# Two of the four weight sums of a feed-forward pair made by adding DMAs from GpSimd

## The chip, the cores and the metric

The kernel runs on one core of one Trainium2 chip. The metric is the device time of one execution in microseconds (us), the median of several runs. The core has TensorE (PE in the rows) for matmuls, VectorE (DVE), ScalarE (ACT), GpSimd (POOL) and SyncE (SP), each with an instruction stream of its own that runs in order; semaphores tie them together. DMAs are issued by SP or, where the text says so, by POOL.

## The reference

A block of layers on x of shape (1, 256, 1024): a first model with two layers (an "even" and an "odd" attention mixer, each followed by a feed-forward network), then one layer of a second model, again with a feed-forward network. The change touches the three feed-forward networks only. Cut to them:

```
D_MODEL, SEQ, D_FF = 1024, 256, 2816        # float32 throughout

def swiglu(h, w1, w3, w2):
    return (jax.nn.silu(h @ w1) * (h @ w3)) @ w2

# layers 0 and 1 of the first model
h = rms_norm(x, norm_ffn_g[layer])
x = x + swiglu(h, ffn_w1[layer], ffn_w3[layer], ffn_w2[layer])
# the layer of the second model
h2 = rmsnorm(x, norm2_w)
x = x + (jax.nn.silu(h2 @ w_ffn_gate) * (h2 @ w_ffn_up)) @ w_ffn_down
```

## The kernel before

**Three products for one.** Every float32 matmul is made as three fp32r matmuls: a weight block W is split into `high` (W rounded to fp32r, written by ScalarE, L719 from the ring `raw` or L724 from a block in `arena`) and `low` (W minus high, written by VectorE, L1167 or L1173), and `three_products` (L1779 to L1781) adds x_high·W_high, x_high·W_low and x_low·W_high. A weight block, a "unit", is 128 partitions x 2048 values, 1 MB, loaded by two DMAs of 512 KB. `high` and `low` have three slots each (RING = 3): the high of a unit may be written when TensorE has done the unit three places ahead of it in the order, and TensorE starts a unit when its low is there (`low_ready`).

**A feed-forward network** has 11 hidden chunks of 256 columns. Chunks 0, 1, 2, 5 and 8 are "plain": two up units U (24 matmuls each). Chunks (3,4), (6,7) and (9,10) are pairs, the FIRST, MIDDLE and LAST one. For a pair the product of two row tiles of x with two chunks, over two halves of the inner dimension, is a 2x2 by 2x2 block product, made with seven products of 12 matmuls each (Winograd's form of Strassen's algorithm) in place of eight. The four weight blocks of a pair are B11 and B12 (upper half of the inner dimension, chunks p and p+1) and B21 and B22 (lower half). They are loaded into X11, X12, X21 and X22 in `arena`, and VectorE makes four sums of them, T1 = B12-B11 (L1337, `t1`), T2 = B22-T1 (L1346, `t2`), T4 = B21-T2 (L1351, `t4`) and T3 = B22-B12 (L1357, `t3`), each over 128 x 2048 values, in the tiles XT1 and XT2. Product P1 uses B11, P2 B21, P3 B22, P4 T4, P5 T1, P6 T2 and P7 T3. Every hidden chunk c also has a down unit D(c) (24 matmuls) with the transpose `hiddenT` of its hidden values ahead of it (ScalarE L833, VectorE L1311).

**What sets the order.** `ffn_order` (L75) gives the order of units for all engines, and each engine's program is written out by hand in that order: `pair_begin`, `pair_end` and `last_pair_end` exist for ScalarE, VectorE and TensorE. On TensorE a pair runs P1, D, P5, D, P6, P2, P3, then U, P7, U, P4; the MIDDLE pair has a further D behind P6, and the LAST pair has no U: it runs P7, D, P4, D, D. Behind a product, ScalarE and VectorE take pieces of the result out of PSUM: `s1` and `s5` copies, `u2` (L1378), `c12` (L1383), `silu_c11` (ScalarE L864) with `gate_c11` (VectorE L1399). The U behind a pair writes the PSUM banks 0 and 1, so TensorE starts its first half only after `gate_c11` and its second after `c12` (`up_after_pair`).

**Loads.** SP issues all weight loads in one written order (`load_ffn`); the loads of the next pair into X11, X21, X12 and X22 each wait for the last reader of the tile. GpSimd issues a few small loads early, and computes reciprocal roots between the networks; during the feed-forward networks it does nothing.

Of the kernel before, what the change touches and what calls it, by code (L numbers as in the profile page):

```python
# [32 lines left out]
P = 128  # L33
# [107 lines left out]
def program(nc, x, norm_mix_g, norm_ffn_g, ev_w_in, ev_w_out, ev_q_norm_g, ev_k_norm_g, ev_pool_w,  # L141
# [59 lines left out]
    with ExitStack() as ctx:  # L201
# [84 lines left out]
        X11, X12, X22, X21, XT1, XT2 = (take(UNIT) for _ in range(6))  # L286
# [82 lines left out]
        x11_in, x12_in, x22_in, x21_in = sem("x11_in"), sem("x12_in"), sem("x22_in"), sem("x21_in")  # L369
        x_copied = sem("x_copied")  # L370
# [157 lines left out]
        def _(sp):  # L528
# [33 lines left out]
            def load_ffn(f):  # L562
# [11 lines left out]
                up_quarter(f, X12, p + 1, 0, x12_in)  # L574
# [4 lines left out]
                for p in PAIRS[:-1]:  # L579
# [54 lines left out]
        def _(pool):  # L634
# [42 lines left out]

            row_rstd(0, 0)
# [10 lines left out]
            for e in (1, 2, 3, 4):  # L689
# [5 lines left out]
                load_gain(NORMS[e + 1], e + 1)  # L695
            head_rstd((4, 5, 6, 7), 8)
# [8 lines left out]
            row_rstd(6, 5)  # L705


        @block.scalar
        def _(act):
# [106 lines left out]
            def ffn(f):  # L816
# [39 lines left out]
                def high_t(p, i):  # L856

                    src, made = {5: (XT1, 1), 6: (XT2, 2), 4: (XT2, 4 if p == LAST_PAIR else 3), 7: (XT1, 3 if p == LAST_PAIR else 4)}[i]
                    act.wait_ge(t_ready, 4 * pair_seq(f, p) + made)
                    block_high(n0 + FFN_AT["P", p, i], src)  # L860
# [9 lines left out]
                def pair_begin(p):  # L870
# [4 lines left out]
                    high_t(p, 5)  # L875
# [6 lines left out]
                    high_t(p, 6)  # L882
                    pair_product_done(p, 5)
                    nc.scalar.activation(f_C22, bank(1), ACT.Copy).then_inc(s5_ready, 1)
                    if p == MIDDLE_PAIR:
                        down(w[2])
                        hiddenT(w[2])
                    high_b21(p)
                    if p == LAST_PAIR:
                        hiddenT(w[2])  # L890
                    high_b22(p)

                def pair_end(p):
# [3 lines left out]
                    high_t(p, 7)  # L897
                    up(p + 2, 1)
                    silu_of(p, f_C12, c12_ready)
                    high_t(p, 4)  # L900
# [6 lines left out]
                def last_pair_end(p):  # L907

                    high_t(p, 7)
                    silu_c11(p)  # L910
                    down(p - 3)
                    high_t(p, 4)
# [247 lines left out]
        def _(dve):  # L1160
# [134 lines left out]
            def ffn(f):  # L1295
# [24 lines left out]
                def low_of(p, i):  # L1320

                    src = {1: X11, 2: X21, 3: X22, 4: XT2, 5: XT1, 6: XT2, 7: XT1}[i]
# [9 lines left out]
                def t1(p):  # L1332
                    dve.wait_ge(x11_in, 32 * pair_seq(f, p) + 32)
                    dve.wait_ge(x12_in, 32 * pair_seq(f, p) + 32)
                    if p > FIRST_PAIR:
                        low_done(p - 3, 7)
                    nc.vector.tensor_tensor(XT1, X12, X11, ALU.subtract).then_inc(t_ready, 1)  # L1337

                def t2(p):
                    dve.wait_ge(x22_in, 32 * pair_seq(f, p) + 32)  # L1340
                    dve.wait_ge(t_ready, 4 * pair_seq(f, p) + 1)
# [4 lines left out]
                    nc.vector.tensor_tensor(XT2, X22, XT1, ALU.subtract).then_inc(t_ready, 1)  # L1346

                def t4(p):
                    dve.wait_ge(x21_in, 32 * pair_seq(f, p) + 32)
                    low_done(p, 6)  # L1350
                    nc.vector.tensor_tensor(XT2, X21, XT2, ALU.subtract).then_inc(t_ready, 1)  # L1351

                def t3(p):

                    dve.wait_ge(t_ready, 4 * pair_seq(f, p) + 2)
                    low_done(p, 5)
                    nc.vector.tensor_tensor(XT1, X22, X12, ALU.subtract).then_inc(t_ready, 1)  # L1357
# [1007 lines left out]
```

## Time and profile before

| | |
|---|---|
| runs | 971.13, 971.67, 971.86 us; median 971.67 |
| the profiled execution | 972.1 us, span from first to last instruction 970.3 us |
| TensorE busy | 960.7 us, 99% of the span, 4644 matmuls; granted clock 1.0 throughout |
| VectorE busy | 761.3 us, 78% |
| ScalarE busy | 546.5 us, 56% |
| GpSimd busy | 42.8 us, 4% |
| DMA | 177.48 MB, 183 GB/s in the mean |

The profile shows one execution. "Busy" of TensorE counts a matmul of 512 columns as some 0.39 us, while the next one starts 0.227 us after it, so short waits hide inside the busy share; a wait of TensorE is read from the distance of two starts. The three networks run at about 95 to 269, 388 to 563 and 792 to 967 us. The three show the same pattern to 0.01 us at the places spoken of below, so rows are shown of the first one.

### The profile page before, as it was taken

The numbers are of one execution on the slowest core, as the hardware profiler recorded it, in microseconds if no ns is written. First come the engines' busy times: TensorE is split into PE (matmuls) and PEld (weight loads), VectorE is DVE, ScalarE is ACT, GpSimd is POOL, SyncE is SP. The second block draws the span as 40 slices with busy tenths as digits, with TensorE's granted clock in tenths as the row PEclk, the third lists the DMA queues.
The fourth block names the chain that finished last, engine by engine and source line by source line (L and its number), as shares of the span: only waits on it lengthen the run. The fifth ranks groups of instructions, "written<-read, shape, count | busy, mean of one in ns | idle before, by whom it ended". The sixth has DMA issues, their size and how long they took to land.

```text
span 970.3 us, 11764 instructions
## 1 busy us (share of the span) xinstructions
PE 960.7 (99%) x4644; PEld 788.8 (81%) x4644; DVE 761.3 (78%) x790; ACT 546.5 (56%) x579; POOL 42.8 (4%) x62
## 2 busy tenths in 40 slices
PE   8999999999999999999999999999999999999998
PEld 6878888888788888888888788888888888888886
DVE  5978879899865777879999885963565678899896
ACT  6556655656555755655555655555344465565662
POOL 2511000000000000000000021000000000000000
PEclk9999999999999999999999999999999999999999
DMA  8643966472374434967472275446435559456511
GB/s 298 256 131 114 354 230 224 149 242 87 107 239 154 149 111 130 314 224 264 132 260 87 87 240 179 168 149 199 154 127 197 165 183 341 155 199 215 187 74 44
DMA packets 112473, 177.48 MB, mean 183 GB/s; under 512 B 6817, under 2 KB 74529, under 8 KB 112418
## 3 DMA queue, kind: packets, MB, share of 16 engines
q1 hardware_dynamic: 110992, 172.73, 53.3%
q0 software_dynamic: 1280, 3.94, 1.2%
q8 instruction: 37, 0.61, 0.3%
q14 instruction: 18, 0.15, 0.0%
q10 hardware_dynamic: 146, 0.07, 0.0%
HBM read 175.66 MB, written 1.05 MB: 182 GB/s over the span
## 4 chain that ended last, share of the span: by engine, by line
PE 85%; DVE 9%; issue 3%; ACT 3%; POOL 0%; DMA 0%; DVEq 0%; ACTq 0%
PE psum L1779 26%; PE psum L1781 25%; PE psum L1780 25%; PE psum L1851 4%; DVE low L1173 4%; DVE low L1167 1%; ACT high L724 1%; DVE arena L1357 1%; DVE arena L1351 1%; DVE arena L1566 1%; PE psum L2183 1%; DVE small L1565 1%; PE psum L1868 1%; ACT high L719 1%; PE psum L2214 1%
## 5 line engine op out<-in xcount | busy, mean ns | idle before, releaser
L1167 DVE TENSOR_TENSOR low<-raw,high 128x2048 fp32r<-128x2048 f32 (+1 forms) x123 | 277.3, 2258 | 106.1 <-ACT high L719 106.0
L1779 PE MATMUL psum<-high,xh 128*128 128x512 f32 x732 | 291.0, 398 | 0.0
L1781 PE MATMUL psum<-high,xl 128*128 128x512 f32 x732 | 285.6, 390 | 0.0
L1780 PE MATMUL psum<-low,xh 128*128 128x512 f32 x732 | 285.1, 390 | 0.0
L719 ACT ACTIVATE high<-raw 128x2048 fp32r<-128x2048 f32 (+1 forms) x125 | 236.2, 1890 | 75.0 <-PE psum L1781 74.1
L1781 PEld LDWEIGHTS psum<-high,xl 128*128 128x128 f32 x732 | 137.4, 188 | 29.4
L1779 PEld LDWEIGHTS psum<-high,xh 128*128 128x128 f32 x732 | 137.5, 188 | 28.3 <-issue 0.7
L1780 PEld LDWEIGHTS psum<-low,xh 128*128 128x128 f32 x732 | 137.7, 188 | 26.8
L1173 DVE TENSOR_TENSOR low<-arena,high 128x2048 fp32r<-128x2048 f32 x63 | 144.0, 2286 | 15.1 <-ACT high L724 15.1
L724 ACT ACTIVATE high<-arena 128x2048 fp32r<-128x2048 f32 x63 | 120.6, 1914 | 43.4 <-PE psum L1781 43.4
L1779 PE MATMUL psum<-high,mh 128*128 128x512 f32 x256 | 103.8, 406 | 1.4 <-DVE low L1173 1.4
L1779 PE MATMUL psum<-high,gh 128*128 128x512 f32 x264 | 103.6, 392 | 0.4
L1781 PE MATMUL psum<-high,gl 128*128 128x512 f32 x264 | 102.9, 390 | 0.0
L1780 PE MATMUL psum<-low,gh 128*128 128x512 f32 x264 | 102.8, 389 | 0.0
L1781 PE MATMUL psum<-high,ml 128*128 128x512 f32 x256 | 100.2, 391 | 0.0
L1780 PE MATMUL psum<-low,mh 128*128 128x512 f32 x256 | 99.8, 390 | 0.0
L833 ACT ACTIVATE gh<-psum 128x512 fp32r<-128x512 f32 x33 | 19.8, 599 | 82.2 <-PE psum L1851 81.8
L1779 PEld LDWEIGHTS psum<-high,mh 128*128 128x128 f32 x256 | 48.1, 188 | 14.1 <-issue 5.0
L1779 PEld LDWEIGHTS psum<-high,gh 128*128 128x128 f32 x264 | 49.6, 188 | 11.7 <-DVE gl L1311 1.6
L1781 PEld LDWEIGHTS psum<-high,gl 128*128 128x128 f32 x264 | 49.6, 188 | 10.4
L1780 PEld LDWEIGHTS psum<-low,gh 128*128 128x128 f32 x264 | 49.6, 188 | 10.1
L1781 PEld LDWEIGHTS psum<-high,ml 128*128 128x128 f32 x256 | 48.0, 188 | 10.7
(183 smaller groups left out, 890.2 us busy)
## 6 DMA issues: line engine op xcount, KB each, us to landing
raw<-in_ffn_w SPq DMA_DIRECT2D x84, 512.0 KB, 5.0
raw<-in_w_in SPq DMA_DIRECT2D x52, 512.0 KB, 4.6
arena<-in_ffn_w SPq DMA_DIRECT2D x48, 512.0 KB, 5.6
raw<-in_od_w_qkv SPq DMA_DIRECT2D x24, 512.0 KB, 4.8
raw<-in_w_ffn_down SPq DMA_DIRECT2D x22, 512.0 KB, 4.5
raw<-in_ev_w_in SPq DMA_DIRECT2D x12, 512.0 KB, 6.4
arena<-in_w_ffn_gate SPq DMA_DIRECT2D x12, 512.0 KB, 5.1
arena<-in_w_ffn_up SPq DMA_DIRECT2D x12, 512.0 KB, 6.1
```

Source lines behind the costliest of these rows:

```text
L719: nc.scalar.activation(high[:, n % RING, 0:cols], raw[:, r, 0:cols], ACT.Copy).then_inc(high_ready, 1)
L724: nc.scalar.activation(high[:, n % RING, :], src, ACT.Copy).then_inc(high_ready, 1)
L833: nc.scalar.activation(gh[:, s % 2], bank(6).rearrange("p (k n) -> p k n", k=2), ACT.Copy).then_inc(gh_ready, 1)
L1167: nc.vector.tensor_tensor(low[:, n % RING, 0:cols], raw[:, RING_AT[n] % RING, 0:cols], high[:, n % RING, 0:cols].bitcast(F32), ALU.subtrac ...
L1173: nc.vector.tensor_tensor(low[:, n % RING, :], src, high[:, n % RING, :].bitcast(F32), ALU.subtract).then_inc(low_ready, 1)
L1351: nc.vector.tensor_tensor(XT2, X21, XT2, ALU.subtract).then_inc(t_ready, 1)
L1357: nc.vector.tensor_tensor(XT1, X22, X12, ALU.subtract).then_inc(t_ready, 1)
L1565: step(nc.vector.max(top8, score))
L1779: nc.tensor.matmul(out, sh, wh, start=start, stop=False, skip_group_check=True)
L1780: nc.tensor.matmul(out, sh, wl, start=False, stop=False, skip_group_check=True)
L1781: return nc.tensor.matmul(out, sl, wh, start=False, stop=stop, skip_group_check=True)
L1851: ins = nc.tensor.transpose(bank(dst_bank, j * P, (j + 1) * P), src, ident)
```

## The change

Of the four sums of a pair VectorE makes two, T2 and T4. T1 and T3 are made by DMAs that GpSimd issues with an adding write: B12 is loaded into XT1 and B11 is added to it from HBM; later, when B22 in X22 has been split for P3 and read for T2, B12 is added to it from HBM, and X22 then holds T3. The signs are turned so that all are sums (T1 = B11+B12, T3 = B22+B12, T2 = B22+T1, T4 = B21+T2), with the signs of the x sums and of the two combining steps c12 and c22 turned to match. The tile X12 is gone. As X22 has to be done with before T3 can be made, P3 comes ahead of P6 and P2: the order is P1, D, P5, D, P3, P2, P6 in the FIRST pair, P3, P2, D, P6 in the MIDDLE pair, and P3, P6, P2 in the LAST pair. SP's load order changes too: X22 of the next pair now waits for the low of P7.

```diff
         w = [("D", c) for c in downs_within(p)]
-        order += [("P", p, 1), w[0], ("P", p, 5), w[1], ("P", p, 6)] + [d for d in w[2:] if p == MIDDLE_PAIR]
-        order += [("P", p, 2), ("P", p, 3)]
+        order += [("P", p, 1), w[0], ("P", p, 5), w[1], ("P", p, 3)]
+        if p == FIRST_PAIR:
+            order += [("P", p, 2), ("P", p, 6)]
+        elif p == MIDDLE_PAIR:
+            order += [("P", p, 2), w[2], ("P", p, 6)]
+        else:
+            order += [("P", p, 6), ("P", p, 2)]
...
-        X11, X12, X22, X21, XT1, XT2 = (take(UNIT) for _ in range(6))
+        X11, X22, X21, XT1, XT2 = (take(UNIT) for _ in range(5))
...
                     load_up(f, p + 2, 0)
-                    after_low("P", p, 5)
+                    load_up(f, p + 2, 1)
+                    after_low("D", p - 1)
                     up_quarter(f, X11, p + 3, 0, x11_in)
-                    load_up(f, p + 2, 1)
+                    up_quarter(f, XT1, p + 4, 0, x12_in)
                     load_down(f, p + 1)
-                    after_low("P", p, 2)
+                    after_low("U", p + 2, 0)
                     up_quarter(f, X21, p + 3, 1, x21_in)
-                    after_low("P", p, 3)
-                    up_quarter(f, X12, p + 4, 0, x12_in)
                     load_down(f, p + 2)
+                    after_low("P", p, 7)
                     up_quarter(f, X22, p + 4, 1, x22_in)
                     load_down(f, p)
...
+            def add_quarter(f, c, block, done):
+
+                block = block.rearrange("p (k c) -> p k c", k=4)
+                for j in range(2):
+                    src = FFN_W[f][j][0:4 * P, c * FC:(c + 1) * FC]
+                    pool.dma_start(block[:, :, j * FC:(j + 1) * FC], src.rearrange("(k p) c -> p k c", p=P), accum_op=ALU.add
+                                   ).then_inc(done, 16)
+
+            def ffn_sums(f):
+                n0 = U_FFN[f]
+                for p in PAIRS:
+                    pool.wait_ge(x12_in, 32 * pair_seq(f, p) + 32)
+                    add_quarter(f, p, XT1, t1_in)
+                    pool.wait_ge(low_ready, n0 + FFN_AT["P", p, 3] + 1)
+                    pool.wait_ge(t_ready, 2 * pair_seq(f, p) + 1)
+                    add_quarter(f, p + 1, X22, t3_in)
...
+                def high_t3(p):
+                    act.wait_ge(t3_in, 32 * pair_seq(f, p) + 32)
+                    block_high(n0 + FFN_AT["P", p, 7], X22)
...
-                nc.vector.tensor_tensor(XT1, X12, X11, ALU.subtract).then_inc(t_ready, 1)
...
-                nc.vector.tensor_tensor(XT1, X22, X12, ALU.subtract).then_inc(t_ready, 1)
```

On VectorE, in the FIRST pair of a network, from the transpose behind D(2) on. L1173 and L1214 are the low of a pair block, L1167 and L1208 the low of a ring unit (here the U behind the pair), L1351 and L1385 are T4, L1357 is T3, L1399 and L1427 `gate_c11`, L1378 and L1406 `u2`. Before:

```order
L1311 TENSOR_TENSOR gl<-psum,gh 128x512
L1173 TENSOR_TENSOR low<-arena,high 128x2048
L1351 TENSOR_TENSOR arena<-arena 128x2048
L1173 TENSOR_TENSOR low<-arena,high 128x2048
L1357 TENSOR_TENSOR arena<-arena 128x2048
L1173 TENSOR_TENSOR low<-arena,high 128x2048
L1167 TENSOR_TENSOR low<-raw,high 128x2048
L1399 SCALAR_TENSOR_TENSOR xn<-psum,small,xn 128x256
L1378 TENSOR_TENSOR xn<-psum,arena 128x512
```

After:

```order
L1352 TENSOR_TENSOR gl<-psum,gh 128x512
L1214 TENSOR_TENSOR low<-arena,high 128x2048 x3
L1385 TENSOR_TENSOR arena<-arena 128x2048
L1208 TENSOR_TENSOR low<-raw,high 128x2048
L1427 SCALAR_TENSOR_TENSOR xn<-psum,small,xn 128x256
L1406 TENSOR_TENSOR xn<-psum,arena 128x512
```

The lows of P3, P2 and P6 now stand in a row, and T4, which stood behind the first low, stands behind all three, right ahead of the low of the U unit and of `gate_c11`.

On VectorE in the LAST pair, from the low of the third product on (L1387 and L1415 are `u3`). Before:

```order
L1173 TENSOR_TENSOR low<-arena,high 128x2048
L1357 TENSOR_TENSOR arena<-arena 128x2048
L1173 TENSOR_TENSOR low<-arena,high 128x2048
L1351 TENSOR_TENSOR arena<-arena 128x2048
L1311 TENSOR_TENSOR gl<-psum,gh 128x512
L1173 TENSOR_TENSOR low<-arena,high 128x2048
L1378 TENSOR_TENSOR xn<-psum,arena 128x512
L1173 TENSOR_TENSOR low<-arena,high 128x2048
L1399 SCALAR_TENSOR_TENSOR xn<-psum,small,xn 128x256
L1167 TENSOR_TENSOR low<-raw,high 128x2048
L1387 TENSOR_TENSOR xn<-psum,arena 128x512
```

After:

```order
L1214 TENSOR_TENSOR low<-arena,high 128x2048 x2
L1352 TENSOR_TENSOR gl<-psum,gh 128x512
L1214 TENSOR_TENSOR low<-arena,high 128x2048
L1385 TENSOR_TENSOR arena<-arena 128x2048
L1406 TENSOR_TENSOR xn<-psum,arena 128x512
L1214 TENSOR_TENSOR low<-arena,high 128x2048
L1427 SCALAR_TENSOR_TENSOR xn<-psum,small,xn 128x256
L1208 TENSOR_TENSOR low<-raw,high 128x2048
L1415 TENSOR_TENSOR xn<-psum,arena 128x512
```

T3 is gone, the lows of P3 and P6 come first, and the low of P2, T4 and `u2` stand between them and the low of P7 (the last L1214).

On GpSimd, behind the reciprocal roots ahead of the first network. Before:

```order
L693 DMA cst<-consts 128x1536
L638 DMA gains<-in_norm_mix_g 128x1024
L650 TENSOR_SCALAR small<-small 128x1
```

After (with the semaphores waited for):

```order
L716 DMA cst<-consts 128x1536 [waits pooled_ready]
L644 DMA gains<-in_norm_mix_g 128x1024 [waits xn_ready]
L689 DMA arena<-in_ffn_w 128x4x256 [waits x12_in]
L689 DMA arena<-in_ffn_w 128x4x256
L689 DMA arena<-in_ffn_w 128x4x256 [waits t_ready,low_ready]
L689 DMA arena<-in_ffn_w 128x4x256
```

Twelve adding DMAs per network are new: two for T1 and two for T3 in each of three pairs.

## Rows read from the trace of the kernel before

**Rows 1.** The page: busy us of each engine (share of the span) xinstructions.

```profile
PE 960.7 (99%) x4644; PEld 788.8 (81%) x4644; DVE 761.3 (78%) x790; ACT 546.5 (56%) x579; POOL 42.8 (4%) x62
```

**Rows 2.** Waits of PE: us in total, times, longest.

```profile
PE psum L1779 <- DVE low L1173: 1.4, 6, 0.3
```

**Rows 3.** Groups by line, VectorE: busy us, mean ns, idle before.

```profile
L1357 DVE TENSOR_TENSOR arena<-arena 128x2048 f32<-128x2048 f32 x9 | 20.6, 2285 | 0.0
```

**Rows 4.** Timeline of PE, FIRST pair: start us, us.

```profile
152.89 0.39 PE L1781 MATMUL psum<-high,xl 128*128 128x512 f32 x1
153.56 0.47 PE L1779 MATMUL psum<-high,mh 128*128 128x512 f32 x1 [0.28 <-DVE low L1173]
...
156.40 0.39 PE L1779 MATMUL psum<-high,xh 128*128 128x512 f32 x1
```

**Rows 5.** Timeline of DVE, FIRST pair.

```profile
142.12 2.29 DVE L1173 TENSOR_TENSOR low<-arena,high 128x2048 fp32r<-128x2048 f32 x1 [1.12 <-ACT high L724]
144.51 2.29 DVE L1351 TENSOR_TENSOR arena<-arena 128x2048 f32<-128x2048 f32 x1
...
151.12 2.28 DVE L1173 TENSOR_TENSOR low<-arena,high 128x2048 fp32r<-128x2048 f32 x1
153.33 2.28 DVE L1167 TENSOR_TENSOR low<-raw,high 128x2048 fp32r<-128x2048 f32 x1
155.53 0.48 DVE L1399 SCALAR_TENSOR_TENSOR xn<-psum,small,xn 128x256 f32<-128x256 f32 x1
```

**Rows 6.** Timeline of ACT, FIRST pair.

```profile
140.17 1.91 ACT L724 ACTIVATE high<-arena 128x2048 fp32r<-128x2048 f32 x1
...
142.93 1.91 ACT L724 ACTIVATE high<-arena 128x2048 fp32r<-128x2048 f32 x1
147.93 1.92 ACT L724 ACTIVATE high<-arena 128x2048 fp32r<-128x2048 f32 x1 [3.09 <-PE psum L1781]
```

**Rows 7.** Timeline of PE, LAST pair.

```profile
238.06 0.48 PE L1779 MATMUL psum<-high,mh 128*128 128x512 f32 x1
...
240.90 0.39 PE L1779 MATMUL psum<-high,xh 128*128 128x512 f32 x1
...
243.97 0.47 PE L1779 MATMUL psum<-high,mh 128*128 128x512 f32 x1 [0.19 <-DVE low L1173]
...
249.61 0.39 PE L1779 MATMUL psum<-high,gh 128*128 128x512 f32 x1
```

**Rows 8.** Timeline of ACT, LAST pair.

```profile
232.96 1.91 ACT L724 ACTIVATE high<-arena 128x2048 fp32r<-128x2048 f32 x1
...
238.34 0.60 ACT L833 ACTIVATE gh<-psum 128x512 fp32r<-128x512 f32 x1 [3.47 <-PE psum L1851]
238.84 1.91 ACT L724 ACTIVATE high<-arena 128x2048 fp32r<-128x2048 f32 x1
```

**Rows 9.** Timeline of DVE, LAST pair.

```profile
243.75 0.68 DVE L1378 TENSOR_TENSOR xn<-psum,arena 128x512 f32<-128x512 f32 x1
244.35 2.28 DVE L1173 TENSOR_TENSOR low<-arena,high 128x2048 fp32r<-128x2048 f32 x1
```

**Rows 10.** Timeline of SP: DMA issues; then DMAs issued at 149 to 150, us to landing.

```profile
149.03 0.93 SPq L548 DMA_DIRECT2D arena<-in_ffn_w  x2
...
arena<-in_ffn_w SPq DMA_DIRECT2D x2, 512.0 KB, 4.5
```

**Rows 11.** Windows: length, PE, PEld, DVE, ACT, POOL busy, PEclk, DMA share, GB/s.

```profile
153.50:154.00 0.50, 0.45 (x2) 0.43 (x3) 0.50 (x1) 0.50 (x2) 0.00 (x0) 1.00 0.33 102
...
235.00:240.00 5.00, 5.00 (x26) 4.14 (x25) 5.00 (x3) 1.66 (x2) 0.00 (x0) 1.00 0.01 6
```

**Rows 12.** Timeline of POOL: two DMA issues.

```profile
25.00 0.81 POOL L670 DMA_DIRECT2D poolw<-in_ev_pool_w  x1
...
93.55 0.63 POOL L693 DMA_DIRECT2D cst<-consts  x1
```

**Rows 13.** Timeline of DVE beside the second of them.

```profile
93.14 2.28 DVE L1167 TENSOR_TENSOR low<-raw,high 128x2048 fp32r<-128x2048 f32 x1
```

More of the change, by code:

```diff
@@ L705, in _ @@
             row_rstd(6, 5)
+            ffn_sums(2)
         @block.scalar
@@ L854, in high_b22, with high_t1, high_t2, high_t4 @@
                     block_high(n0 + FFN_AT["P", p, 3], X22)
[L856 to L860, printed above, removed]
+                def high_t1(p):
+                    act.wait_ge(t1_in, 32 * pair_seq(f, p) + 32)
+                    block_high(n0 + FFN_AT["P", p, 5], XT1)
+                def high_t3(p):
+                    act.wait_ge(t3_in, 32 * pair_seq(f, p) + 32)
+                    block_high(n0 + FFN_AT["P", p, 7], X22)
+                def high_t2(p):
+                    act.wait_ge(t_ready, 2 * pair_seq(f, p) + 1)
+                    block_high(n0 + FFN_AT["P", p, 6], XT2)
+                def high_t4(p):
+                    act.wait_ge(t_ready, 2 * pair_seq(f, p) + 2)
+                    block_high(n0 + FFN_AT["P", p, 4], XT2)
                 def silu_c11(p):
@@ L1345, in t2 @@
                         dve.wait_ge(sums_low, f + 1)
-                    nc.vector.tensor_tensor(XT2, X22, XT1, ALU.subtract).then_inc(t_ready, 1)
+                    nc.vector.tensor_tensor(XT2, X22, XT1, ALU.add).then_inc(t_ready, 1)
                 def t4(p):
@@ L1350, in t4 @@
                     low_done(p, 6)
[L1351 to L1356, printed above, removed]
-                    nc.vector.tensor_tensor(XT1, X22, X12, ALU.subtract).then_inc(t_ready, 1)
+                    nc.vector.tensor_tensor(XT2, X21, XT2, ALU.add).then_inc(t_ready, 1)
                 def x_sums():
@@ L1367, in x_sums @@
                     dve.wait_ge(prep_step, at + 4)
-                    nc.vector.tensor_tensor(a22, a21, a22, ALU.add).then_inc(prep_step, 1)
+                    nc.vector.tensor_tensor(a22, a21, a22, ALU.subtract).then_inc(prep_step, 1)
                     nc.vector.tensor_tensor(a21, a11, a21, ALU.subtract).then_inc(prep_step, 1)
@@ L1372, in x_sums @@
                     dve.wait_ge(prep_step, at + 7)
-                    nc.vector.tensor_tensor(a12, a12, a11, ALU.subtract).then_inc(prep_step, 1)
+                    nc.vector.tensor_tensor(a12, a12, a11, ALU.add).then_inc(prep_step, 1)
                 def u2(p):
@@ L1382, in c12 @@
                     dve.wait_ge(u2_ready, pair_seq(f, p) + 1)
-                    nc.vector.tensor_tensor(f_C12, bank(1), f_C12, ALU.add).then_inc(c12_ready, 1)
+                    nc.vector.tensor_tensor(f_C12, bank(1), f_C12, ALU.subtract).then_inc(c12_ready, 1)
                 def u3_and_c22(p):
@@ L1389, in u3_and_c22 @@
                     dve.wait_ge(s5_ready, pair_seq(f, p) + 1)
-                    nc.vector.tensor_tensor(f_C22, f_C21, f_C22, ALU.add).then_inc(c22_ready, 1)
+                    nc.vector.tensor_tensor(f_C22, f_C22, f_C21, ALU.subtract).then_inc(c22_ready, 1)
                 def c21(p):
@@ L1966, in pair_begin, with product_2, product_6 @@
                         hiddenT(w[2])
-                        pe.wait_ge(c21_ready, g)
-                    product(p, 6, bank(7), sum_tile(2), True, False)
-                    if p == MIDDLE_PAIR:
-                        down(w[2])
-                    pe.wait_ge(s1_ready, g + 1)
-                    product(p, 2, bank(0), x_tile(0, 1), False, True)
                     pe.wait_ge(s5_ready, g + 1)
                     product(p, 3, bank(1), sum_tile(4), False, True)
+                    if p == LAST_PAIR:
+                        product_6(p)
+                        product_2(p)
+                    else:
+                        product_2(p)
+                        if p == MIDDLE_PAIR:
+                            down(w[2])
+                        product_6(p)
+                def product_2(p):
+                    pe.wait_ge(s1_ready, pair_seq(f, p) + 1)
+                    product(p, 2, bank(0), x_tile(0, 1), False, True)
+                def product_6(p):
+                    if p > FIRST_PAIR:
+                        pe.wait_ge(c21_ready, pair_seq(f, p))
+                    product(p, 6, bank(7), sum_tile(2), True, False)
                 def product_7(p):
```

75 lines of the change are left out of this document (34 added, 41 removed).

## The prediction

> **What bounds the kernel now.** I read the page first: TensorE is busy 960.7 of 970.3 us, VectorE 761.3, ScalarE 546.5, GpSimd 42.8 [rows 1]. So no time is to be had but what TensorE waits. The waits list gives its waits for weight lows: six, 1.4 us together, and all on VectorE's L1173 [rows 2]. Since a matmul counts as 0.39 us of busy time but the next starts 0.227 us after it, I took the cost from the timeline of starts. In the FIRST pair the last matmul of P2 starts at 152.89, P3 only at 153.56: 0.44 us more than the step of 0.227, and P3 then takes 2.84 us (to 156.40) where 12 steps are 2.72, another 0.12 for starting up after a wait [rows 4]. In the LAST pair P2 starts at 240.90 and P3 at 243.97, 3.07 where 2.72 would do: 0.35 us [rows 7]. Both come back in each of the three networks (hence six waits). All that the change can win in the pairs is thus 0.56 + 0.47 or so per network, 3.1 us in all, however much work leaves VectorE. What matters is whether the new order makes TensorE wait elsewhere.
>
> **What is removed.** T1 and T3 leave VectorE: 18 instructions, of which the nine of T3 take 2.285 us each, 20.6 us [rows 3]; those of T1 have the same shape. That is about 41 us of VectorE, but beside TensorE's work: directly it is worth only the waits above. The turned signs change no instruction's count or shape: nothing.
>
> **The FIRST pair after the change.** TensorE's times up to the end of D(2) stay as they are, since the order up to there does. D(2) is done at 147.93, which is when ScalarE may write the high of the third unit behind it [rows 6]. Before, that unit was P2; now it is P6. I follow the chain with the steps that the rows show. High of P6: 147.93 + 1.92 = 149.85. VectorE starts a low 0.04 after the high (140.17 + 1.91 to 142.12) [rows 5, 6]: 149.89. T4 overwrites the block just read, so it waits for that low to be complete: it starts 2.39 us behind it (142.12 to 144.51) [rows 5], at 152.28. The low of the next U starts 2.21 later, at 154.49, and gate_c11 2.20 later, at 156.69, and takes 0.48 (steps 151.12, 153.33, 155.53) [rows 5]: 157.17. U writes bank 0, which gate_c11 reads, so TensorE starts it some 0.16 us behind that (as P3 started at 153.56 behind a low that ended at 153.40) [rows 4, 5]: at 157.33. Without a wait TensorE would have been there at 152.89 + 0.23 (end of the second product behind D(2)) + 2.72 = 155.84 [rows 4]. P3 itself no longer waits: its high takes the place at 142.93 [rows 6], its low is over by 147.2, half a microsecond ahead of TensorE. But U waits, 1.5 us. Before, U started at 156.40 [rows 4]: 0.93 us later now, and 0.12 for starting up behind a wait: **+1.05 us**. What is queued behind T4 on VectorE is just what TensorE asks for next; before the change T4 stood two instructions earlier, in a gap. The work behind this place (u2, c12, low of P7) ends by 160.8, TensorE is at P7 at about 162.9: no second wait.
>
> **The MIDDLE pair.** D(3) stands between P2 and P6, another 5.4 us of cover. The same counting gives the low of U(8,0) ready some 1.8 us ahead of TensorE. Nothing.
>
> **The LAST pair.** P7 follows straight on the three products. TensorE would reach it at 238.06 + 2.84 + 2 x 2.72 = 246.34 [rows 7]. Its low needs two things.
> One is VectorE's queue. The high of P2 stands behind the copy of a transpose (238.34) and is written from 238.84 to 240.75, as before [rows 8]; low of P2 from 240.79, T4 from 243.0, u2 from 245.2, and the low of P7 0.60 behind u2 (243.75 to 244.35) [rows 9], at 245.8. It ends at 248.1 and P7 starts at 248.25: a wait of 1.9 us even if T3 is there in time. T4 sits ahead of a low that TensorE needs first; before, the low of P7 followed u2 at 244.35 and its product followed P3 unhindered.
> The other is T3. Its adding DMAs may start when the low of P3 is made: high from 232.96 to 234.87 [rows 8], low to 237.2. Call the lag the time from there to the landing of both DMAs; the high and low of P7 and the step to TensorE then add 0.04 + 1.92 + 0.04 + 2.28 + 0.16 = 4.44. P7 starts at the later of 248.25 and 241.64 plus the lag; the first holds up to a lag of 6.6.
>
> **The lag of an adding DMA pair** is in no row. Near end: the same 1 MB as plain loads from SP, two DMAs issued in 0.93 us from 149.03, with 4.5 us to landing each, traffic falling off at 153.5 to 154.0 [rows 10, 11], so about 5.0 us; GpSimd needs 0.81 us to issue one DMA of 128 x 4 pieces [rows 12] where SP needs less, 2 x 0.81 - 0.93 = 0.7 us more for the pair: a lag of 5.7. Far end: an adding write has to fetch the old value too, so the engines would move every byte twice; the stretch of traffic in the rows was some 3.8 us long (149.03 plus about a microsecond to its fall-off), and a second 3.8 gives 9.5. Below 5.7 it cannot go, as nothing makes the adding kind cheaper than the plain one. At 235 to 240 the DMA engines are idle (share 0.01) [rows 11], so no queue is added. I take 8, nearer to the far end, since the second fetch goes through the same engines. P7 then starts at 249.6, and D(6) 2.84 later, at 252.5, where it was 249.61 [rows 7]: **+2.9 us**. D(6)'s own high follows T3's on ScalarE and its low is over at about 252.1, just ahead. Behind it the order is unchanged and the delay passes on to the end.
>
> **The rest of the adding DMAs.** T1 has long cover: B12 of the FIRST pair lands at about 115, T1's high is written at 131.5 and T2 at 135.6; in the other pairs the distance is over 15 us. T3 of the FIRST pair may start at 147.2 and is needed for a high by about 158, of the MIDDLE one more. The 18 MB more of traffic fall mostly into gaps, but 100 to 128 us is full already, so D(1), X22 and D(2) land later by up to 4 us; their users come 5 us or more after them before. I put nothing on it and keep it for the upper end.
>
> The page "SBUF — State Buffer" of the Trainium skill (the box on how VectorE blocks DMAs of GpSimd) says that GpSimd cannot write its descriptors while VectorE runs an instruction that takes both ports, and that a tensor_tensor takes only the read side. In this trace GpSimd issued a DMA at 93.55 in 0.63 us in the middle of a VectorE low that ran from 93.14 to 95.42 [rows 12, 13]: no blocking seen, which agrees with the second half. By the first half alone, the issue at 237.2 would wait for the low of P6 behind it; that case is priced below.
>
> **Sum.** Per network 1.05 + 2.86 = 3.9, times three 11.7 us; the profiled execution of 972.1 would become 983.8. The median of the runs is 0.4 below the profiled one, so **983.4 us**.
>
> **Rivals.**
> (a) T3 lands within 6.6 us. VectorE's queue sets P7, and D(6), whose high stands behind silu_c11 of the now later P2, costs 0.3 more: 1.05 + 1.8 per network, 980.2. For it: the near end. Against: the second fetch. Chance 0.14.
> (b) Forecast, a lag from 6.6 to 9.5: 980.2 to 987.9. Chance 0.58.
> (c) Blocking by VectorE: GpSimd's issue waits for a low, 2.2 us more of lag in each LAST pair, 6.6 us in all: 990. Against it stands the issue at 93.55 [rows 12, 13]. Chance 0.05. The page of the Trainium skill named above is where a blocking of this kind is described.
> (d) The adding write is slow by itself, with a lag of 12. LAST pair +6.9; in the FIRST pair P7 would wait as well, 147.2 + 12 + 4.4 = 163.6 against 162.9: 0.7. With 1.05 that is 8.6 per network, 26 us: 997. Nothing speaks for it but that no row shows such a DMA. Chance 0.14.
> (e) The other side: faster. If VectorE, with 41 us taken off, had run ahead at both places, only the old waits would go: 3.1 us, 968.6. It decides on whether the low of P7 in the LAST pair ends by 246.2; the chain above puts it at 248.1, and its start is tied to TensorE's own D(8), not to VectorE's load, so lighter load does not help. Chance 0.04.
> (f) About no change: one of the two waits is as I say and the other is not there. Chance 0.05.
>
> **How the numbers follow.** The likeliest is (b), 983.4. The range from 978.5 (a with a microsecond and a half of error) to 992 (c, and part of d) leaves out (e), (f) and most of (d). About 0.2% is what a measurement of this kernel can tell from no change. Slower by more: a, b, c, d, 0.91; within: 0.05; faster: 0.04.
>
> **What would show it.** In the profile after: VectorE's busy time about 41 us less; TensorE waiting at the U behind the FIRST pair's P6 for gate_c11, 1.5 us, and at P7 of the LAST pair, 1.9 us or more, three times each; no wait at P3. The DMAs on GpSimd's queue show the lag directly. If P7's wait ends with VectorE's queue, it is (a); if ScalarE idles until the DMA lands, (b) to (d). I am wrong if P7 of the LAST pair does not wait, or if TensorE waits near the start of a network for D(1), T1 or X22.

## The result: slower by 2.1%, nearly twice what was forecast

| | before | after |
|---|---|---|
| median | 971.63 us (971.13 to 971.86) | 992.69 us (990.33 to 993.32) |
| profiled execution | 972.1 us, span 970.3 us | 993.3 us, span 991.5 us |

The ratio is 1.0214 (95% interval 1.0202 to 1.0226). The forecast was 983.4 us, 11.7 us more than before, with a range up to 992.0; measured are 21.1 us more. The direction and the two places were right; the size was not, and the median lies 0.7 us above the range.

**The page of the kernel after**: the span, busy us of each engine, and two of its lines in 40 slices.

```profile
span 991.5 us, 11773 instructions
...
PE 966.9 (98%) x4644; PEld 793.8 (80%) x4644; DVE 724.1 (73%) x772; ACT 545.8 (55%) x579; POOL 90.1 (9%) x98
...
PEclk9999999999899999999999899999999999999999
```

VectorE lost 37.2 us of busy time against [rows 1] and the kernel is longer by 21. TensorE has the same 4644 matmuls and 6.2 us more of busy time. That is strange for equal work, and the clock line gives the reason: in two slices it stands at 8 where the clock was full throughout before.

**The waits of TensorE after**: us in total, times, longest.

```profile
PE psum L1797 <- DVE low L1214: 12.5, 3, 4.3
PE psum L1797 <- DVE xn L1427: 4.0, 3, 1.3
```

The six short waits of [rows 2] have become three of 4 us and three of 1.3 us. They are the two places of the prediction, once each in every network.

**The FIRST pair after**, timeline of TensorE (start us, us). It runs 0.19 us ahead of the trace of before at the start of the first network, so 0.19 is to be added when the two are compared.

```profile
155.42 0.39 PE L1799 MATMUL psum<-high,ml 128*128 128x512 f32 x1
157.13 0.47 PE L1797 MATMUL psum<-high,xh 128*128 128x512 f32 x1 [1.32 <-DVE xn L1427]
```

And VectorE at that place:

```profile
149.70 2.29 DVE L1214 TENSOR_TENSOR low<-arena,high 128x2048 fp32r<-128x2048 f32 x1 [0.53 <-ACT high L752]
152.10 2.29 DVE L1385 TENSOR_TENSOR arena<-arena 128x2048 f32<-128x2048 f32 x1
154.31 2.29 DVE L1208 TENSOR_TENSOR low<-raw,high 128x2048 fp32r<-128x2048 f32 x1
156.51 0.48 DVE L1427 SCALAR_TENSOR_TENSOR xn<-psum,small,xn 128x256 f32<-128x256 f32 x1
```

TensorE's last matmul of P6 starts at 155.42 and U at 157.13, 1.71 us later instead of 0.227: a wait of 1.48. T4 (L1385) stands ahead of the low of U and of `gate_c11` (L1427), and TensorE waits for the latter. The U starts 0.92 us later than in [rows 4], the 0.19 counted in, and with 0.11 for starting up behind the wait, all that follows it comes 1.03 us later.

**The LAST pair after**, ScalarE and GpSimd from the low of P3 on:

```profile
239.68 1.91 ACT L752 ACTIVATE high<-arena 128x2048 fp32r<-128x2048 f32 x1
247.25 1.91 ACT L752 ACTIVATE high<-arena 128x2048 fp32r<-128x2048 f32 x1 [5.67 <-DMA arena<-in_ffn_w]
```

```profile
238.32 2.57 POOL L689 DMA_DIRECT2D arena<-in_ffn_w  x2 [39.59 <-DVE low L1214]
```

VectorE there:

```profile
235.74 4.49 DVE L1214 TENSOR_TENSOR low<-arena,high 128x2048 fp32r<-128x2048 f32 x2 [3.12 <-ACT high L752]
...
241.62 2.29 DVE L1214 TENSOR_TENSOR low<-arena,high 128x2048 fp32r<-128x2048 f32 x1 [0.79 <-ACT high L752]
243.82 2.28 DVE L1385 TENSOR_TENSOR arena<-arena 128x2048 f32<-128x2048 f32 x1
246.03 0.68 DVE L1406 TENSOR_TENSOR xn<-psum,arena 128x512 f32<-128x512 f32 x1
249.19 2.29 DVE L1214 TENSOR_TENSOR low<-arena,high 128x2048 fp32r<-128x2048 f32 x1 [2.48 <-ACT high L752]
```

The first of the two lows that start at 235.74 (P3's) is over at 238.02. GpSimd begins to issue T3's two adding DMAs at 238.32 and needs 2.57 us for it. ScalarE stands still until they have landed, at 247.25: a lag of 9.2 us. VectorE is done with `u2` at 246.7 and waits too, so it is not its queue that sets P7 but the DMA.

TensorE there:

```profile
246.95 0.39 PE L1799 MATMUL psum<-high,xl 128*128 128x512 f32 x1
251.63 0.77 PE L1797 MATMUL psum<-high,mh 128*128 128x512 f32 x1 [4.29 <-DVE low L1214]
...
253.05 0.63 PE L1797 MATMUL psum<-high,mh 128*128 128x512 f32 x1
...
254.33 0.63 PE L1797 MATMUL psum<-high,mh 128*128 128x512 f32 x1
...
256.89 0.63 PE L1797 MATMUL psum<-high,gh 128*128 128x512 f32 x1
```

P7 starts at 251.63, after a wait of 4.45 us (4.39 and 4.18 in the other two networks). The part that the prediction does not have comes next. From 253.05 to 254.33 there are three matmuls, 0.43 us each, where the step was 0.227. P7 takes 5.26 us, to 256.89, and not 2.84. The windows over this stretch (length; PE, PEld, DVE, ACT, POOL busy; PEclk; DMA share; GB/s) say why:

```profile
245.00:250.00 5.00, 2.34 (x11) 1.60 (x9) 2.52 (x3) 2.75 (x3) 0.00 (x0) 1.00 0.34 54
250.00:252.50 2.50, 0.87 (x2) 0.80 (x3) 2.50 (x3) 2.50 (x2) 0.00 (x0) 0.64 0.00 0
252.50:255.00 2.50, 2.50 (x7) 1.92 (x7) 1.57 (x1) 0.62 (x1) 0.00 (x0) 0.50 0.00 0
255.00:257.50 2.50, 2.50 (x7) 1.92 (x7) 0.37 (x1) 0.00 (x0) 0.00 (x0) 0.50 0.80 244
257.50:260.00 2.50, 2.50 (x13) 2.04 (x12) 2.47 (x4) 1.24 (x3) 0.00 (x0) 0.99 0.45 175
```

TensorE's granted clock (PEclk) is full (1.00, that is 2.4 GHz) up to 250, falls while the engine stands waiting for P7, stays at 0.50 (1.2 GHz) until about 257.5 and is full again from there. The Trainium skill ("TensorE: Matmul & The Clock Gate", Part 1: The HAM clock gate) gives this clock gate two states, 1.2 and 2.4 GHz, with the lower one for an idle engine and 426.7 ns from start to start of 512 columns there; the trace agrees, with 0.43 us.

**Where the 21 us are.** Read from the distances between TensorE's starts, in the LAST pair from the first matmul of the three products into D(6), summed over the three networks:

| | us |
|---|---|
| FIRST pair, wait for `gate_c11` and starting up (3 x 1.03) | 3.1 |
| LAST pair, as forecast with a lag of 8 (3 x 2.86) | 8.6 |
| LAST pair, P7 later than that (1.15, 1.1, 0.9) | 3.1 |
| P7 and the start of D(6) at half clock (2.75, 2.3, 1.6) | 6.6 |
| sum; difference of the spans | 21.4; 21.2 |

The last two rows are what the forecast lacked. The last one was a claim so far: the half clock could also be there without the wait. The experiments were made for that, and for the lag.

### The profile page after: what moved, and what is told of

Same layout as the page of the kernel before. It is cut to its first block, busy times and chain, and to the rows that moved or that the text cites. A ratio compares the mean times of both kernels' runs of the same rounds, so it can differ in the third digit from the quotient of the medians.

```text
span 991.5 us, 11773 instructions
## 1 busy us (share of the span) xinstructions
PE 966.9 (98%) x4644; PEld 793.8 (80%) x4644; DVE 724.1 (73%) x772; ACT 545.8 (55%) x579; POOL 90.1 (9%) x98
## 3 DMA queue, kind: packets, MB, share of 16 engines
HBM read 194.53 MB, written 1.05 MB: 197 GB/s over the span
## 4 chain that ended last, share of the span: by engine, by line
PE 85%; DVE 7%; ACT 3%; DMA 3%; issue 1%; POOL 1%; ACTq 0%; DVEq 0%
PE psum L1797 26%; PE psum L1799 25%; PE psum L1798 25%; PE psum L1869 4%; DVE low L1214 2%; DVE low L1208 2%; ACT high L752 2%; DMA arena<-in_ffn_w 2%; DMA arena<-in_w_ffn_up 1%; DVE arena L1584 1%; PE psum L2212 1%; DVE small L1583 1%; PE psum L1886 1%; ACT high L747 1%; PE psum L2243 1%
## 5 line engine op out<-in xcount | busy, mean ns | idle before, releaser
L1208 DVE TENSOR_TENSOR low<-raw,high 128x2048 fp32r<-128x2048 f32 (+1 forms) x123 | 277.3, 2258 | 106.7 <-ACT high L747 106.6
L1214 DVE TENSOR_TENSOR low<-arena,high 128x2048 fp32r<-128x2048 f32 x63 | 143.5, 2290 | 58.7 <-ACT high L752 58.6
L1797 PE MATMUL psum<-high,mh 128*128 128x512 f32 x256 | 106.0, 414 | 12.5 <-DVE low L1214 12.5
L1798 PE MATMUL psum<-low,mh 128*128 128x512 f32 x256 | 102.4, 400 | 0.0
L1799 PE MATMUL psum<-high,ml 128*128 128x512 f32 x256 | 102.3, 400 | 0.0
L1799 PEld LDWEIGHTS psum<-high,gl 128*128 128x128 f32 x264 | 49.7, 188 | 10.5
```

What stands on the lines that cost most here:

```text
L1208: nc.vector.tensor_tensor(low[:, n % RING, 0:cols], raw[:, RING_AT[n] % RING, 0:cols], high[:, n % RING, 0:cols].bitcast(F32), ALU.subtrac ...
L1214: nc.vector.tensor_tensor(low[:, n % RING, :], src, high[:, n % RING, :].bitcast(F32), ALU.subtract).then_inc(low_ready, 1)
L1797: nc.tensor.matmul(out, sh, wh, start=start, stop=False, skip_group_check=True)
L1798: nc.tensor.matmul(out, sh, wl, start=False, stop=False, skip_group_check=True)
L1799: return nc.tensor.matmul(out, sl, wh, start=False, stop=stop, skip_group_check=True)
```

## The experiments

Each is compared with the kernel before, timed beside it on the same chip (971.26 or 971.32 us). The diffs are against the kernel after.

### No adding DMAs in the LAST pair

```diff
                     pool.wait_ge(low_ready, n0 + FFN_AT["P", p, 3] + 1)
+                    if p == LAST_PAIR:
+                        continue
...
                 def high_t3(p):
-                    act.wait_ge(t3_in, 32 * pair_seq(f, p) + 32)
+                    if p < LAST_PAIR:
+                        act.wait_ge(t3_in, 64 * f + 32 * PAIRS.index(p) + 32)
```

> The changed kernel without the two adding DMAs of T3 in the LAST pair of each network (P7 there uses B22 instead of T3: that part of the computation is left out). Theory: the wait of 4.4 us ahead of P7 is the lag of these DMAs (9.2 us from the low of P3 to landing), and behind them stands VectorE's queue (low of P2, T4, u2) at 1.9 us. So P7's wait falls to 1.9 us, not to nothing. If TensorE's clock stays at full speed after so short a wait, the time is 971.6 + 3 x (1.05 + 1.6) = 979.6 us; if it falls as it does after 4.4 us, some 8 us more, 987.5. Rival (the adding DMAs cost something elsewhere, P7's wait is VectorE's): the wait stays above 3 us and the time above 989.

Measured: 979.57 us, ratio 1.0087 (1.0072 to 1.0102). Its waits of TensorE, and P7's start in the first network:

```profile
PE psum L1800 <- DVE low L1217: 5.2, 3, 1.7
PE psum L1800 <- DVE xn L1430: 4.0, 3, 1.3
```

```profile
246.07 0.39 PE L1802 MATMUL psum<-high,xl 128*128 128x512 f32 x1
248.18 0.47 PE L1800 MATMUL psum<-high,mh 128*128 128x512 f32 x1 [1.72 <-DVE low L1217]
248.49 0.40 PE L1801 MATMUL psum<-low,mh 128*128 128x512 f32 x1
```

With T3 never late, P7 still waits, 2.11 - 0.227 = 1.88 us: this is VectorE's queue (low of P2, T4, `u2`), which the prediction put at 1.9. The mean clock is 1.0 and the steps behind the wait are 0.23 again. So the adding DMAs of this one pair cost 13.1 us in three networks (992.69 - 979.57), the half clock included. The other 8.3 us over the kernel before are the FIRST pair's 3.1 and some 1.8 per network in the LAST pair: the wait of 1.88, another of 0.22 ahead of D(6), less the 0.35 that P3 used to wait.

### The same DMAs as plain writes

```diff
-            def add_quarter(f, c, block, done):
+            def add_quarter(f, c, block, done, add=True):
...
-                    pool.dma_start(..., accum_op=ALU.add
+                    pool.dma_start(..., **({"accum_op": ALU.add} if add else {})
...
-                    add_quarter(f, p + 1, X22, t3_in)
+                    add_quarter(f, p + 1, X22, t3_in, add=p < LAST_PAIR)
```

> The changed kernel with T3's two DMAs of the LAST pair as plain writes from the same queue instead of adding ones (P7 there uses B12 instead of T3: the addition is left out). Theory: a part of the lag of 9.2 us is the second fetch of the adding write; the plain pair lands some 2.5 to 3.5 us sooner (lag 5.7 to 6.7), P7's wait falls from 4.4 to about 2 us, and the time is as that of the run without these DMAs, 980 to 988 us depending on the clock. Rival (the lag is the issue by GpSimd, 2.6 us, and the load itself; adding costs nothing): the lag stays above 8.5 us and the time at 992 to 993.

Measured: 980.35 us, ratio 1.0095 (1.008 to 1.011). GpSimd's issue and the high of P7 in the first network, and from the DMA view of 238 to 241 us the time to landing:

```profile
238.38 1.55 POOL L689 DMA_DIRECT2D arena<-in_ffn_w  x2 [40.13 <-DVE low L1214]
```

```profile
244.16 1.92 ACT L752 ACTIVATE high<-arena 128x2048 fp32r<-128x2048 f32 x1 [2.52 <-DMA arena<-in_ffn_w]
```

```profile
arena<-in_ffn_w POOLq DMA_DIRECT2D x2, 512.0 KB, 4.7
```

The same view of the kernel after has

```profile
arena<-in_ffn_w POOLq DMA_DIRECT2D x2, 512.0 KB, 7.2
```

The low of P3 ends at 238.07 here and the block is there at 244.16: a lag of 6.1 us. The near end of the prediction, 5.7 from SP's loads and an issue of 0.81 per DMA, was good for the plain kind. Adding makes it 9.2. GpSimd needs 2.57 instead of 1.55 us to issue the pair, but data already flows while it issues, so this delays the start of the traffic by only 0.5 us (from 239.75 to 240.25). The other 2.5 us are a longer transfer: the traffic lasts from 240.25 to 246.5 where the plain pair's lasts from 239.75 to 243.5. One microsecond from the middle of each, the adding pair first (columns as in the windows above):

```profile
242.00:243.00 1.00, 1.00 (x6) 0.84 (x5) 1.00 (x1) 0.00 (x0) 0.00 (x0) 1.00 1.24 199
```

```profile
242.00:243.00 1.00, 1.00 (x6) 0.82 (x5) 1.00 (x1) 0.00 (x0) 0.00 (x0) 1.00 1.01 344
```

The DMA engines are no less busy and move 199 GB/s in place of 344. That fits the second fetch of the prediction, but the fetch itself is in no trace. The two kinds also differ in their packets, 1056 against 288 for the same 1 MB; SP's plain pair of [rows 10] has 1055 packets and runs at some 385 GB/s, so their number alone does not halve the rate on SP's queue.

The other thing to read here is that a lag of 6.1 costs nothing in the LAST pair: it is as long as with no DMA at all (to 0.04 us), since VectorE's queue holds P7 back as long. P7 again waits 1.88 us, at full clock. Between the two traces there are 0.8 us as between the medians, and all of them lie ahead of the first network, which the edit does not touch. The step from here to the kernel after, 3.1 us of lag, costs 12.3 us.

### TensorE kept running through the wait

```diff
                 def last_pair_end(p):
+                    pe.wait_ge(gl_ready, down_seq(f, p - 3) + 1)
+                    for i in range(18):
+                        nc.tensor.matmul(bank(6), xh[:, 0, 0:P], xh[:, 2 * (i % 4):2 * (i % 4) + 2, :].rearrange("p k n -> p (k n)"),
+                                         start=True, stop=True, skip_group_check=True)
                     product_7(p)
```

> The changed kernel with 18 matmuls of no use (512 columns each, into a bank that is free) ahead of P7 in the LAST pair of each network, 18 x 0.227 = 4.1 us, while TensorE would wait for T3. Theory: the half clock behind the wait (0.43 us a matmul for 12 to 14 matmuls) comes from TensorE having stood still; kept busy it stays at full clock, P7 starts at the same time, and the loss of 2.9, 2.7 and 2.0 us in the three networks goes: 992.7 - 7.6 = 985 us. Rival (the clock falls for another reason, as the DMAs or the place in the program): the half clock stays, and the time is 992 to 994.

Measured: 985.64 us (985.21 to 986.13), ratio 1.0149 (1.0134 to 1.0164). Timeline of TensorE and a window of the same place (this trace runs 1.15 us ahead of the one of after):

```profile
246.02 4.24 PE L2023 MATMUL psum<-xh 128*128 128x512 f32 x18
250.25 0.47 PE L1797 MATMUL psum<-high,mh 128*128 128x512 f32 x1
...
253.06 0.39 PE L1797 MATMUL psum<-high,gh 128*128 128x512 f32 x1
```

```profile
250.00:252.50 2.50, 2.50 (x12) 1.92 (x11) 2.50 (x3) 1.74 (x1) 0.00 (x0) 1.00 0.00 0
```

This is the run that settles the clock. P7 starts as late as in the kernel after (0.2 us earlier, counted from the start of the pair, in two networks and 0.2 later in the third), VectorE, ScalarE and the DMAs do the same work, and 54 matmuls whose result nobody uses have been added. Yet it is 7.05 us shorter, because P7 now takes 2.81 us (250.25 to 253.06; 2.84 and 2.81 in the other networks) and not 5.26, 5.14 and 4.41. The table above had 6.6 for this. The half clock is thus a result of TensorE's standing still, and it is a third of the whole loss.

### T4 of the FIRST pair behind `c12`

```diff
+                    sp.wait_ge(t_ready, 2 * pair_seq(f, p) + 2)
                     up_quarter(f, X21, p + 3, 1, x21_in)
...
                         low_of(p, 6)
-                        t4(p)
+                        if p > FIRST_PAIR:
+                            t4(p)
...
                     c12(p)
+                    if p == FIRST_PAIR:
+                        t4(p)
                     low_of(p, 7)
```

> The changed kernel with T4 of the FIRST pair moved on VectorE from ahead of the U unit's low to behind c12, ahead of the low of P7 (SP's load into X21 waits for it). Theory: the wait of TensorE ahead of the U unit, 1.5 us with 0.1 for starting up, three times, is T4 in front of the U's low and gate_c11; it goes, and nothing is late in its place: 992.7 - 3 x 1.6 = 987.9 us. Rival: something else is late by nearly as much (low of P7 or the reload of X21), the wait moves and the time stays above 991.

Measured: 990.28 us (988.71 to 991.78), ratio 1.0191 (1.0174 to 1.0208): the median is 2.4 us below that of after, half of what was expected. The runs of the two kernels overlap (988.7 to 991.8 against 990.3 to 993.3), so the size of the gain is known only roughly; what the edit does is read from the trace. The waits and the FIRST pair of its first network:

```profile
PE psum L1801 <- DVE low L1215: 14.5, 6, 4.1
```

```profile
159.84 0.39 PE L1803 MATMUL psum<-high,xl 128*128 128x512 f32 x1
161.32 0.47 PE L1801 MATMUL psum<-high,mh 128*128 128x512 f32 x1 [1.09 <-DVE low L1215]
```

The wait of U for `gate_c11` is gone from the list, so its cause is shown: T4's place. But a wait of 1.25 us (0.79 in the other networks) stands one unit later, at P7 of the FIRST pair. T3 is late there as well. In the kernel after that was hidden, since U came late itself: the low of P7 is over at 161.99 there and P7 starts at 162.68. These are GpSimd and ScalarE of the kernel after:

```profile
147.27 2.55 POOL L689 DMA_DIRECT2D arena<-in_ffn_w  x2 [29.58 <-DVE low L1214]
150.35 2.56 POOL L689 DMA_DIRECT2D arena<-in_ffn_w  x2 [0.53 <-DMA arena<-in_ffn_w]
```

```profile
157.75 1.92 ACT L752 ACTIVATE high<-arena 128x2048 fp32r<-128x2048 f32 x1 [4.15 <-DMA arena<-in_ffn_w]
```

T3 is issued at 147.27 and ScalarE has it at 157.75, 10.5 us later. The windows over the two lags (columns as before) show what is different:

```profile
147.50:157.50 10.00, 8.68 (x39) 6.92 (x38) 9.37 (x6) 4.32 (x3) 4.88 (x4) 1.00 1.18 257
238.00:247.00 9.00, 9.00 (x44) 7.39 (x42) 7.92 (x6) 2.40 (x2) 2.57 (x2) 1.00 0.78 117
```

In the FIRST pair the DMA engines move 257 GB/s, SP's loads and GpSimd's next pair (from 150.35) among them, in the LAST one 117, nothing but T3. So of the 1.6 us per network that U's wait and start had cost, 1.25 are lost again at P7 in the first network and 0.79 in the others. In the LAST pair this kernel is slower: P7 takes 5.26, 5.25 and 5.26 us, all of it at half clock, where it took 5.26, 5.14 and 4.41 in the kernel after, 1.0 us more. By the two traces the edit is thus worth only 0.5 us in the networks; another 1.0 of the 1.5 us between them lies ahead of the first network, which it does not touch.

### The LAST pair as before

T3 is made by VectorE again (as T2 - B11, which the turned signs allow without B12), P3 goes last, and VectorE, ScalarE and TensorE have the order of before in this pair. Orders and waits of the other engines left out, the edit is

```diff
+                def t3_last(p):
+                    dve.wait_ge(t_ready, t_seq(f, p) + 1)
+                    low_done(p, 5)
+                    nc.vector.tensor_tensor(XT1, XT2, X11, ALU.subtract).then_inc(t_ready, 1)
...
-                    low_of(p, 3)
                     if p == LAST_PAIR:
                         low_of(p, 6)
-                        hiddenT(w[2])
+                        t3_last(p)
                         low_of(p, 2)
                         t4(p)
+                        hiddenT(w[2])
                     else:
+                        low_of(p, 3)
                         low_of(p, 2)
...
+                    low_of(p, 3)
                     u2(p)
```

> The changed kernel with the LAST pair in the order of before (P6, P2, P3, P7) and its T3 made by VectorE as T2 - B11 into XT1, in the place where VectorE made T3 before; the FIRST and MIDDLE pair as changed. Theory: all that the LAST pair costs (wait ahead of P7, half clock, late D(6)) goes back to the 0.35 us wait ahead of P3; left is the FIRST pair's 1.05 us per network: 971.3 + 3.2 = 974.5 us. Rival (the adding DMAs of T1 and of T3 in the other pairs, 14 MB more of traffic, cost something of their own): 977 or more.

Measured: 973.86 us, ratio 1.0033 (1.002 to 1.0045). Its waits:

```profile
PE psum L1816 <- DVE xn L1444: 4.0, 3, 1.3
...
PE psum L1816 <- DVE low L1226: 0.8, 4, 0.2
```

Against the kernel without adding DMAs in the LAST pair this is 5.7 us less, about the three times 1.8 that VectorE's queue had cost there. What the median is over the kernel before, 2.5 us, is the FIRST pair's wait, put at 3.1.

The profiled execution is the slowest of the five (975.41 us), and it shows two things more. In the first network P7 of the FIRST pair, whose order this edit leaves alone, waits 0.39 us for its low (the fourth wait of the last line). In the second network T1 comes late:

```profile
427.65 1.92 ACT L758 ACTIVATE high<-arena 128x2048 fp32r<-128x2048 f32 x1 [2.36 <-DMA arena<-in_ffn_w]
```

```profile
436.95 0.50 PE L1816 MATMUL psum<-high,gh 128*128 128x512 f32 x1 [0.82 <-DVE gl L1364]
```

The high at 427.65 is T1's. GpSimd issued its two adding DMAs from 409.40 on, and the DMA view gives 14.8 us to landing. What stands behind it on VectorE is late in turn, and TensorE waits 0.97 us for the transpose at D(2).

### Both places undone

The edits of the last two experiments together.

> As the run before, and T4 of the FIRST pair behind c12 on VectorE. Theory: the U unit's wait of 1.5 us goes, but P7 is asked for 1.5 us sooner and then waits for T3's adding DMAs, 0.8 to 1.25 us as in the run with T4 later; per network 1.05 - 1.6 + 0.9 = 0.35 over before: 972.4 us. Rival: as T4 alone gave only 2.4 us of the 4.8 expected for another reason, 973.5 or more.

Measured: 972.66 us, ratio 1.002 (1.001 to 1.003). Its waits for a low, in the networks:

```profile
PE psum L1820 <- DVE low L1227: 2.7, 6, 0.9
```

Three of these six waits are P7 of the FIRST pair (0.90 us in the first network, at 161.52, and 0.63 in the others): T3 by DMA is late there even now. So even with both orders mended the kernel is 1.3 us over the one before.

### A version that beats both

T1 by adding DMAs in all pairs, T3 by them only in the MIDDLE pair, where another down unit stands in between. In the FIRST and LAST pair T3 = T2 - B11 on VectorE, into a tile of its own, with the orders of before; T4 of the FIRST pair behind the low of P7, T4 of the LAST one in two halves, the second behind the low of D(6).

```diff
+                    if p != MIDDLE_PAIR:
+                        continue
                     pool.wait_ge(low_ready, n0 + FFN_AT["P", p, 3] + 1)
...
+                def t3_last(p):
+                    dve.wait_ge(t_ready, t_seq(f, p) + 1)
+                    nc.vector.tensor_tensor(XT3, XT2, X11, ALU.subtract).then_inc(t_ready, 1)
...
+                def t4_half(i):
+                    c = slice(i * 1024, (i + 1) * 1024)
+                    nc.vector.tensor_tensor(XT2[:, c], X21[:, c], XT2[:, c], ALU.add).then_inc(t_ready, 1)
...
                     low_of(p, 7)
+                    if p == FIRST_PAIR:
+                        t4(p)
```

> T1 by adding DMAs in all pairs, T3 by adding DMAs in the MIDDLE pair only; in the FIRST and LAST pair VectorE makes T3 as T2 - B11 into a tile of its own, with the orders of before on TensorE and ScalarE. The room that T1 left on VectorE is used: T4 of the FIRST pair stands behind the low of P7, T4 of the LAST pair is made in two halves, the second behind the low of D(6). Theory: TensorE's wait ahead of P3 goes in both pairs (0.56 and 0.35 to 0.47 us per network): 971.3 - 3 x 0.9 = 968.6 us. Rival (T4 now late for P4, or the reload of X21 behind it): a wait at P4 or at the transpose ahead of it, and 971 to 973 us.

Measured: 968.47 us (967.86 to 969.85), ratio 0.9973 (0.9963 to 0.9982): faster than the kernel before by 2.9 us. Its page, and all its waits of TensorE for a low:

```profile
PE 959.3 (99%) x4644; PEld 789.3 (82%) x4644; DVE 736.4 (76%) x781; ACT 545.6 (56%) x579; POOL 74.3 (8%) x86
```

```profile
PE psum L2106 <- DVE low L1227: 0.6, 1, 0.6
```

The one wait that is listed lies ahead of the networks. VectorE has 25 us less to do than before instead of 37, and the kernel is 24 us faster than the one with 37. It wins what [rows 2], [rows 4] and [rows 7] had to give: 3.07 us in the networks by the two traces, against the 3.1 us that the prediction named as all there was.

## The prediction against the runs

- **Only TensorE's waits count, 3.1 us are to be won in the pairs: right.** Taking 37 us off VectorE brought nothing by itself; the version without any waits in the networks came to 968.47, the rival (e) was put at 968.6. VectorE's own loss was 37.2 where I had 41; a part of that is that queued sums start every 2.20 us, not every 2.285, and the rest I have not traced.
- **FIRST pair, +1.05 by a wait of 1.5 us for `gate_c11` behind T4: right.** Measured +1.03 with 1.48 us, and shown by moving T4. (The high that waited at 147.93 in the kernel before was P3's and not P2's, as the prediction has it; the chain does not use it.) **"No second wait" was right by its outcome and wrong by its reason**: T3's DMA was nearly as late as TensorE was, and without the first wait the second one shows (1.25, 0.79, 0.79 us). I had the low of P7 over by 160.8 with TensorE there at 162.9; it was over at 162.2, 0.7 us ahead, and in one network of the kernel with the LAST pair as before it was 0.39 us late. I had T3 "needed for a high by about 158" and the high was written from 157.75, as soon as T3 was there. The kernel before has no row for the lag of such a DMA beside other traffic, and I had taken the one lag for both pairs.
- **MIDDLE pair, nothing: right. T1, D(1) and X22 never late: right for TensorE in the kernel after, but "T1 has long cover" was wrong.** No wait of that kind is in its list. Yet T1's adding DMAs, issued at 115.03 in full traffic (307 GB/s up to 131.6), were there only at 131.63, 16.6 us later, and ScalarE had waited 0.26 us for them. With the LAST pair as before, ScalarE waited 2.36 us in the second network and TensorE 0.97. T1 stands at the edge, then, and a run can lose a microsecond by it. I had put nothing on it.
- **LAST pair, floor of 1.9 us by VectorE's queue: right**, 1.88 us with T3 out of the way, and 0.22 ahead of D(6) where rival (a) had 0.3.
- **The lag, "I take 8" between 5.7 and 9.5: the term that was sized too low.** It was 9.2, near the far end, which is 3.1 us in all. The bounds held. Of the 3.1 us by which it is above a plain pair's 6.1, 2.5 are the longer transfer, for which I had a second 3.8; the reason I gave (the old value is fetched too) fits but is not shown. Some 0.5 come from issuing on GpSimd, which I had taken as equal for both kinds.
- **"P7 then starts at 249.6, and D(6) 2.84 later": the step that failed.** I gave P7 the duration that it has behind running matmuls. Behind a wait of over 4 us TensorE's clock was at half, and P7 took 5.26, 5.14 and 4.41 us. That was 6.6 us by the trace of after and 7.05 by the run that filled the wait. With it, and the lag as measured, the sum would have been about 983.4 + 3.1 + 6.6 = 993.1 against 992.69. With the lag right and no term for the clock I would have come to 986.5. The range missed the time for want of this term: it reached 992 only by rivals that were not what happened.
- **The rivals.** (a) is what a plain DMA does: 980.35 measured, 980.2 said, and the lag there was 6.1 us, under the limit of 6.6. (c) is excluded: GpSimd began to issue at 238.32, 0.3 us behind the low that it waited for, while VectorE was at the next low until 240.23. It took 2.57 us, no more than the pair at 115.03 (2.66 us), beside which VectorE stood idle for half the time. (d), a slow adding write, came partly true: not 12 us but 9.2, and 10.5 from the issue in the FIRST pair. For T1, on which no rival had a price, it was 16.6. A time near 992 would have fitted (c) at 990 rather well, from the wrong cause, which is why the traces had to be read and not just the time.

## What to carry to other kernels

Work taken off an engine that is not the bound was worth only the waits of the engine that is (3.1 us here, for 37 us of VectorE). Add those up first, since they are the whole prize, and then look for what the new path makes late, in every place where it is used and beside the traffic of that place. A lag of 3 us more cost 12 us here, as a long wait was paid twice, once as the wait and again as TensorE's slow clock after it. Where such a wait can't be removed, matmuls without a use in its place can win back the second part; here they won 7 us.

## What was not expected of the hardware

- A TensorE that stood still for 4.1 to 4.45 us ran P7 partly or wholly at 1.2 GHz, which cost 1.6 to 2.75 us more each time in the kernel after. After waits of 1.48 and 1.88 us the clock stayed full. In the third network of the kernel after the clock fell only when P7 was already running: P7's first matmul at 963.31 took 0.47 us, the steps grew to 0.43 us from 964.48 on, and the product took 4.41 us. What decides the moment I have not explained. It differs from run to run as well. The four runs of the kernel after have mean clocks of 0.991, 0.991, 0.993 and 0.995 and times of 993.3, 993.2, 992.2 and 990.3 us, and with T4 later 0.99, 0.99, 0.993 and 0.995 go with 991.8, 991.0, 989.6 and 988.7. The three kernels without the fall that have four runs each spread over only 0.7 to 0.9 us. Of the nine runs of the kernel with both places undone eight lie between 972.4 and 973.2 at a clock of 1.0, and the ninth, 975.8 us, has 0.998: it has lost clock somewhere too, though its trace was not kept.
- An adding DMA pair of 2 x 512 KB in pieces of 1 KB: 2.57 us to issue on GpSimd (a plain one 1.55), and 9.2 us from the end of the low it waits for to the data, with DMA engines otherwise idle (plain 6.1). The rate in the middle of the transfer is 199 GB/s (plain 344). Beside other traffic it was 10.5 us from the first issue to the use of the data (257 GB/s in all) and 16.6 us (307 GB/s).
